# A blocked recurrence loop with its copies in another order, its last inversion product in the next group and its masks behind the solution's copy

## What is computed

```python
def step(S, inp):
    r_t, w_t, k_t, v_t, ma_t, b_t = inp
    sa = jnp.einsum('dbhij,dbhj->dbhi', S, ma_t)
    S = S * w_t[..., None, :] + sa[..., None] * b_t[..., None, :] + v_t[..., None] * k_t[..., None, :]
    return S, jnp.einsum('dbhij,dbhj->dbhi', S, r_t)
s_last, ys = lax.scan(step, s0, xs)
```

## Time and profile before

| | us |
|---|---|
| median of 3 runs | 2169.68 |
| lowest, highest | 2169.28, 2173.42 |
| the profiled execution | 2169.53 |
| its span in the trace | 2167.7 |
| its mean granted TensorE clock | 0.924 of full |

### The profile page before, as it was taken

The page is one execution under the profiler, slowest core; times in us unless marked ns, Lnnn a source line. Parts: engine busy times, 40 slices in busy tenths (PEclk is TensorE's granted clock), DMA queues, the critical chain, the costliest instruction groups (busy, mean ns, idle before and its releaser), DMA issues. The chain is left out here.

```text
span 2167.7 us, 55496 instructions
## 1 busy us (share of the span) xinstructions
PE 1842.1 (85%) x24160; PEld 1149.9 (53%) x24160; DVE 1038.4 (48%) x1685; ACT 633.9 (29%) x1233; POOL 524.9 (24%) x596
## 2 busy tenths in 40 slices
PE   6289577789999468999988379799999999999988
PEld 1234476335555258888888244355545455554533
DVE  8789566420888724555545644332221222212276
ACT  0511244322555323444444213231112121120202
POOL 0510000232111024555544433231202121120110
PEclk9589699889999779999999679899999999999999
DMA  6574332511344443333343222211111121111122
GB/s 232 218 210 174 122 110 80 182 43 41 118 151 152 140 156 96 105 103 101 95 143 91 100 100 98 107 57 60 40 39 40 39 78 39 40 39 39 40 74 92
DMA packets 172362, 215.87 MB, mean 100 GB/s; under 512 B 41035, under 2 KB 127051, under 8 KB 170447
## 3 DMA queue, kind: packets, MB, share of 16 engines
q1 hardware_dynamic: 172244, 214.18, 29.9%
HBM read 151.63 MB, written 60.42 MB: 98 GB/s over the span
## 5 line engine op out<-in xcount | busy, mean ns | idle before, releaser
L89 PE MATMUL psum<-arena 128*128 128x384 bf16 (+1 forms) x2028 | 711.5, 351 | 71.2 <-PEq L500 14.7
L90 PE MATMUL psum<-arena 128*128 128x384 bf16 (+1 forms) x2028 | 710.9, 351 | 0.0
L91 PE MATMUL psum<-arena 128*128 128x384 bf16 (+1 forms) x2028 | 710.2, 350 | 0.0
L1625 PE MATMUL psum<-arena 64*64 64x64 f32 x9216 | 347.5, 224 | 39.2 <-issue 32.6
L89 PEld LDWEIGHTS psum<-arena 128*128 128x128 bf16 x2028 | 201.1, 99 | 267.5 <-issue 41.2
L1625 PEld LDWEIGHTS psum<-arena 64*64 64x64 f32 x9216 | 312.4, 136 | 56.4 <-issue 51.3
L1619 PE MATMUL psum<-arena 64*64 64x64 f32 (+2 forms) x6336 | 286.5, 238 | 56.6 <-DMA arena<-xrec 38.5
L91 PEld LDWEIGHTS psum<-arena 128*128 128x128 bf16 x2028 | 201.3, 99 | 178.9 <-issue 9.0
L90 PEld LDWEIGHTS psum<-arena 128*128 128x128 bf16 x2028 | 201.3, 99 | 171.8 <-issue 7.6
L1619 PEld LDWEIGHTS psum<-arena 64*64 64x64 f32 x6336 | 245.5, 135 | 63.5 <-issue 60.8
L1752 ACT ACTIVATE arena<-psum 128x192 f32<-128x192 f32 (+2 forms) x624 | 173.3, 334 | 293.5 <-PE psum L1625 186.8
(11 more groups left out here) (274 smaller groups left out, 2006.2 us busy)
## 6 DMA issues: line engine op xcount, KB each, us to landing
arena<-in_w_ff SPq DMA_DIRECT2D x16, 2048.0 KB, 7.8
arena<-in_w_ada SPq DMA_DIRECT2D x12, 2048.0 KB, 8.4
arena<-xrec SPq DMA_DIRECT2D x72, 320.0 KB, 3.3
arena<-s_tab SPq DMA_DIRECT2D x8, 1600.0 KB, 7.4
x<-arena SPq DMA_DIRECT2D x18, 512.0 KB, 2.6
xrec<-arena SPq DMA_DIRECT2D x4, 2304.0 KB
arena<-xrec SPq DMA_DIRECT2D x72, 128.0 KB
arena<-x SPq DMA_DIRECT2D x18, 512.0 KB, 3.3
```

Source lines behind the costliest of these rows:

```text
L89: nc.tensor.matmul(out, whi, xhi, start=first, stop=False)
L90: nc.tensor.matmul(out, wlo, xhi, start=False, stop=False)
L91: return nc.tensor.matmul(out, whi, xlo, start=False, stop=last)
L1625: done = nc.tensor.matmul(out[half[1 - h]], lhs[half[h]], rhs[half[h]], start=first, stop=last)
```

## The change

It has three parts, though the few words for it name only the first.

1. ACT's copies of a level (1 to 4) go X of direction 0, X of direction 1, transpose of direction 0, transpose of direction 1, where they were X, transpose, X, transpose.
2. `update(5)` is gone. A new step `inverse()` stands in the next body right after `right_side(0)` and ahead of `start(0)`: 12 `heads` products (two directions, three chunks, two heads) into bank SUM, and one ACT copy of 128x384 for both directions in place of two of 128x192. `start(d)` now waits for `q_read` of level 5 and `xt` of level 4; `inverse` also waits for `lt`.
3. DVE's mask of the late matrices moves. For chunk 1 it stays in `right_side(0)`; for chunk 2 and chunk 0 of the next group it now stands in `solve(1)` and `solve(2)`, behind the copy of u.

```diff
@@ order
         if recur:
             f.right_side(0)
+            f.inverse()
...
             f.between(5)
-            f.update(5)
@@ PE
                         if j == 0:
-                            for d in D2:
-                                pe.wait_ge(ev("xt", LEVELS, d), ic)
+                            pe.wait_ge(ev("inv"), ic)
...
                         if recur:
-                            pe.wait_ge(ev("xt", LEVELS, d), ic)
+                            pe.wait_ge(ev("q_read", LEVELS, d), ic)
+                            pe.wait_ge(ev("xt", LEVELS - 1, d), ic)
...
+                    def inverse():
+                        for d in D2:
+                            pe.wait_ge(ev("ready"), 1)
+                            pe.wait_ge(ev("q_read", LEVELS, d), ic)
+                            pe.wait_ge(ev("xt", LEVELS - 1, d), ic)
+                        if chain:
+                            for d in D2:
+                                pe.wait_ge(ev("lt", d), ia)
+                        for d in D2:
+                            for j in G3:
+                                at = 2 * CK + CHAIN * d + CK * j
+                                last = heads(ps[:, SUM, at:at + CK], qs[d][:, j], xx[d][:, 1, j])
+                        last.then_inc(ev("xq", LEVELS), 1)
@@ ACT
                         for d in D2:
                             act.wait_ge(ev("xq", l, d), ia)
-                            if l < LEVELS:
-                                copy(pair(d)[:, 0], ps[:, CROSS[d], 0:CHAIN]).then_inc(ev("x", l, d), 1)
-                                copy(pair(d)[:, 1], ps[:, STAY[d], 0:CHAIN]).then_inc(ev("xt", l, d), 1)
-                            else:
-                                if recur:
-                                    act.wait_ge(ev("u", GROUP - 1), ic)
-                                copy(inv[d].rearrange("p j c -> p (j c)"), ps[:, STAY[d], 0:CHAIN]).then_inc(ev("xt", l, d), 1)
+                            copy(pair(d)[:, 0], ps[:, CROSS[d], 0:CHAIN]).then_inc(ev("x", l, d), 1)
+                        for d in D2:
+                            copy(pair(d)[:, 1], ps[:, STAY[d], 0:CHAIN]).then_inc(ev("xt", l, d), 1)
+
+                    def inverse():
+                        act.wait_ge(ev("xq", LEVELS), ic)
+                        copy(both_inv, ps[:, SUM, 2 * CK:2 * CK + 2 * CHAIN]).then_inc(ev("inv"), 1)
@@ DVE
                     def right_side(j):
-                        nxt = (j + 1) % GROUP
-                        if late0 if nxt == 0 else True:
-                            Part.late(nxt)
+                        if j == 0:
+                            Part.late(1)
...
                         nc.vector.tensor_copy(flat(u), ps[:, OFF, 2 * CK:4 * CK]).then_inc(ev("u_read", j), 1)
+                        if j == 1:
+                            Part.late(2)
+                        if j == 2 and late0:
+                            Part.late(0)
```

More of the change, by code:

```diff
@@ L1385, in stage_recurrence @@
     early = A.take(GROUP, 2, 2, CK)
+    CHAIN = GROUP * CK
     mt = [A.take(2, 5, CK) for _ in G3]
@@ L1390, in stage_recurrence @@
     xx = [A.take(2, GROUP, CK) for _ in D2]
-    inv = [A.take(GROUP, CK) for _ in D2]
+    both_inv = A.take(2 * CHAIN)
+    inv = [both_inv[:, d * CHAIN:(d + 1) * CHAIN].rearrange("p (j c) -> p j c", j=GROUP) for d in D2]
     qs = [A.take(GROUP, CK) for _ in D2]
@@ L1399, in stage_recurrence @@
     flat = lambda v: v.rearrange("p d c -> p (d c)")
-    CHAIN = GROUP * CK
     LATE, OFF, SUM = 4, 6, 7
@@ L1591, in update @@
                         pass
+                    def inverse():
+                        pass
                     def advance(j):
@@ L1730, in update @@
                                 at = slice(j * CK, j * CK + CK)
-                                if l < LEVELS:
-                                    across(ps[:, CROSS[d], at], xx[d][:, 1, j], qs[d][:, j])
+                                across(ps[:, CROSS[d], at], xx[d][:, 1, j], qs[d][:, j])
                                 last = heads(ps[:, STAY[d], at], qs[d][:, j], xx[d][:, 1, j])
                             last.then_inc(ev("xq", l, d), 1)
+                    def inverse():
[11 more added lines that the diff above has]
+                        last.then_inc(ev("xq", LEVELS), 1)
                     def early():
```

## The result

| | before | after |
|---|---|---|
| median of 6 runs each, us | 2170.39 | 2147.83 |
| lowest, highest | 2169.28, 2176.47 | 2137.70, 2152.80 |
| the profiled execution | 2169.53 | 2147.13 |
| its span | 2167.7 | 2145.3 |
| first u copy of the trace | 787.63 | 795.60 |

What follows compares the result with a forecast made beforehand. PE, busy 15.46 of a 16.97 us period, executes in order and idles where its queue's head waits. 22 turns x 0.6 + 21 masks x 0.8 - 1.4 = 28.6 us; 2169.5 - 28.6 = 2141 us, range 2134 to 2150 (chance 0.75).

Steps and rivals of the forecast that it cites:

- The turn: At the loop's turn, update(5) becoming inverse() lets right_side(0) start earlier: 0.6 us less per turn, 0.3 to 0.75.
- The mask of chunk 2: Behind u's copy in solve(1), it frees DVE for between(2)'s adds, so update(2) starts 0.8 us earlier, 0.61 to 0.85.
- the adds run from 909.80: At between(2), DVE's identity adds start at 909.80, behind the first product group's end at 909.77, without the mask ahead.
- The mask of chunk 0: Behind u's copy in solve(2), it delays between(4)'s adds, but advance(2) covers that: 0, upper bound 0.4 us.
- The order of the copies: On ACT, direction 1's X comes earlier, but PE has other products in front or gains little: 0, bound 0.2 us a period.
- How often: Over the recurrence, 22 turns at 0.6 and 21 masks at 0.8 count, less 1.4 lost at a load: 28.6 us.
- The yrec loads: The two loads issued at 1109.57 hold right_side(2), so that group's 0.6 + 0.8 us is lost; wait grows to about 3.5.
- Half of it: Rival: either the turn gives nothing (2153.5 us) or the displaced mask holds the new state (2157 us); chance 0.12.
- Loads: Rival: right_side(2) waits for its load in each period, keeping up to 0.8 us of it: 2153 us; chance 0.03.
- The copies alone: Rival: moved products and masks are hidden anyway, only ACT's copy order matters: 2165 to 2170 us; chance 0.04, with all hidden.
- Slower: PE's clock: Rival: new waits bring 1.2 GHz into steady periods, about 8 us each; six such periods give 2189 us; chance 0.04.
- What would show it: Trace signs: period 15.6 us, no PE idle over 0.2 ahead of update(2), right_side(0) within 0.3 of between(5), two waits grow.

Runs made afterwards that it cites:

- e1: Kernel before with only update(5) turned into inverse(), masks and ACT's copies as before; 2159.49 us, ratio 0.9953.
- e2: Kernel before with only DVE's masks moved; 2154.81 us, ratio 0.9939.
- e10: Kernel after with the mask of chunk 0 put back in right_side(2), ahead of u's copy; 2146.27 us, ratio 0.9887.
- e12: Kernel after with the new order of ACT's copies at level 3 alone, the old order at levels 1, 2 and 4; 2149.10 us, ratio 0.9893.
- e8: Kernel after, unchanged, traced and timed once more; 2147.38 us, ratio 0.9891.
- e4: Kernel after with ACT's copies back in the old order at all levels; 2147.57 us, ratio 0.9894.
- e5: Kernel after with the two yrec loads issued one each behind the first load_step in the last column tile's first two groups; 2141.51 us, ratio 0.9863.
- e3: Kernel before with only the order of ACT's copies changed; 2168.11 us, ratio 0.9998.
- e7: Kernel before with the yrec loads split over two groups and the large loads spread over the first tile's six groups; 2162.68 us, ratio 0.9967.
- e9: Kernel after with the new order of ACT's copies at level 4 only, the old order at levels 1 to 3; 2149.56 us, ratio 0.9903.
- e11: Kernel after with inverse()'s one 128x384 copy as two of 128x192; 2148.53 us, ratio 0.9906.

## Why the prediction was right, and where it was off

**The period** was forecast at 15.6 and is 15.56: 1.41 saved instead of 1.40. But its terms were off in ways that cancel: 0.2 too much for the mask, 0.22 too little for the order of the copies. That the period comes out to 0.04 is in part luck.

**The turn**, taken at 0.6 (0.3 to 0.75), is 0.62 alone (e1). Its steps: `right_side(0)` was to come 0.22 behind `between(5)` and comes 0.24 behind it (0.35 with the old copies); from there to u of chunk 0 was put at 3.16 (919.44 to 922.6) and is 3.19 (903.21 to 906.40).

**The mask of chunk 2**, taken at 0.8 (0.61 to 0.85), is 0.60 (e2). The step that failed is "the adds run from 909.80". That took the end of the last product's record of `between(2)` as the moment from which DVE could start, which made the first add 3.61 behind u of chunk 0; in e2 it is 908.48 - 904.59 = 3.89. In after the last product of that half of `between(2)` ends, by its record, at 909.79, and the add, with DVE idle in front of it, starts at 910.10. Behind `between(1)` this distance is 0.04. At `between(2)` the 64x192 products of `right_side(1)` stand directly ahead in PE's queue, and the last of them ends, by its record, only at 909.92. The profile says that ends of products are modelled, and the Trainium skill (Perfetto Trace Analysis, Summary: the profiler window per engine type) states that for TensorE the reported end is an estimate and the semaphore's way is not in it; the 0.31 here beside 0.04 there is in line with it. That the wider products make the difference is not shown, as no run moved them. The rows before had a sign of it: the mask, with 1.62 of idle in front, waited for products that stand ahead of `between(2)` in PE's queue, and it began only at 909.95, so the adds behind those products could hardly have begun at 909.80. `update(2)` therefore comes (908.95 - 904.59) 4.36 behind u of chunk 0 in e2, where 4.14 was forecast and 4.95 stood before. Two signs were in the prediction's own text: u itself was put only 0.66 earlier, and the lower bound of 0.61 was the measured idle, which is what came.

**The mask of chunk 0**, taken at 0: right (e10, 15.55 beside 15.56; e2 has its third stretch at 7.59 beside 7.58).

**The order of the copies**, taken at 0 with 0.2 as the bound: wrong, 0.10 alone and 0.22 with the rest. The step that failed is "at update(1), (2) and (4) it has right_side(1), advance(1) or early in front". For `update(4)` that looked at PE's products alone; the change had brought the branch of the loop right behind `between(5)`, and a branch waits until the sequencer has handed out everything ahead of it. At `update(3)` the same text found the 0.1 to 0.2 and rounded it to nothing; e12 has 0.11.

**How often.** By the prediction, the 23 periods between the first u copies shrink by 28.6: 0 in the first, 1.4 in each of 20, 0 at the yrec loads, 0.6 in the last. Measured between the two traces: 0.80 in the first, 1.35 in the second, 18 x 1.405 = 25.3 in the steady ones, 1.25 in the last but one; and against it -2.46 at the yrec loads (19.09 to 21.55) and -1.03 in the last (19.19 to 20.22). Sum 25.2; the lengths in the table give 25.3. The last period lies between 19.0 and 20.8 in the traces of all kernels, in no order, and stays open. Outside the recurrence the pair of traces lost 8.0 ahead of it and gained 5.1 behind it, by code that is the same in both: 25.3 - 8.0 + 5.1 = 22.4, the difference of the spans. The 5.1 goes with the granted clock (84 us at 1.2 GHz behind in before, 74 in after); the 8.0 stays open.

**The yrec loads** are the term that was sized wrongly. The wait was forecast to grow to about 3.5 and is 3.63; that it comes so close is luck, since the same kernel has 4.00 in e8, and others with the same gains have 3.07 to 4.76. What was not forecast is that the granted clock is then 1.2 GHz for a while. A windows view of after behind the wait, to be held against 1109.88 to 1128.97 of before, where the clock is 1.00 all through:

```profile
1103.30:1107.00 3.70, 3.70 (x91) 3.51 (x93) 0.00 (x0) 0.61 (x2) 0.00 (x0) 0.50 0.02 5
```

```profile
1109.88:1128.97 19.09, 15.50 (x648) 14.60 (x648) 8.67 (x27) 7.20 (x27) 8.77 (x20) 1.00 0.68 221
```

PE is busy for 17.65 us in this period of after instead of 15.3. The period is 5.99 longer than a steady one: 3.63 of wait and these 2.4. The Trainium skill (TensorE: Matmul & The Clock Gate, HAM oscillation — how this bites in real kernels) says that waits for transfers between bursts of products let the clock fall, so that the next burst starts slow; the trace of after agrees, while e4 had a wait of 3.10 and kept its clock (see the last section). e5, which takes the wait away, takes the slow stretch away too.

**The rivals.** "Half of it" did not come: both halves were there (e1, e2). "Loads" did not: right_side(2) has no idle ahead of it in a steady period. "The copies alone" fell with e3, which can't be told from before. "Slower: PE's clock" put the danger in the steady periods, and there the clock is 1.00; the rule about short idles that it names from the Trainium skill (TensorE: Matmul & The Clock Gate, A second HAM failure mode: psum-queue depth-cycling) is not borne out by the idles of this case. The lower clock appeared at the long wait, where the sum had set 0. One reading in that rival is wrong: the clock did not fall behind the idle of 5.02. In before it was at 1.2 GHz already ahead of this idle, which begins at 801.2:

```profile
797.20:801.00 3.80, 2.92 (x77) 2.92 (x77) 1.22 (x5) 0.83 (x3) 0.74 (x2) 0.50 1.03 418
```

**What would show it.** The period, the adds, the idle ahead of `update(2)` and the start of `right_side(0)` came as stated, but u stands 0.53 behind the first add and not 0.7. Of the two waits that were to grow, the second did; the first shrank from 5.02 to 4.37, while a gap in written-out code some 7 us ahead of it grew from 2.80 to 3.40, so that the two together stayed (7.82 and 7.77).

## What to carry to other kernels

When an engine that works in order is some 90% busy, look for the few idles at the head of its queue and take them away one by one. Each was worth about what the trace showed as idle: the mask 0.60 for 0.61, the turn 0.62 for 0.50 and 0.22, of which 0.24 stayed. Take the shown idle as the value, and the end of a TensorE record as a bound only. When a step is moved across the turn of a loop, ask again what the sequencer must hand out before the branch; and when a kernel gets faster, its waits for loads that don't move can grow (here from 2.08 to between 3.07 and 4.76), and may cost clock besides, so move those loads too.

## What the runs showed of the hardware that was not expected

- Behind the wait for the yrec loads, which every kernel but e5 to e7 has, the granted clock falls or doesn't, and not by the length of the wait alone. The third column is the mean granted clock in the 8 us from the end of the wait (windows view), the fourth the length of the period less that of a steady one:

| wait of PE, us | kernel | granted clock behind it | the period is longer by |
|---|---|---|---|
| 2.08 | before | 1.00 | 2.12 |
| 2.16 | e3 | 0.79 | 3.48 |
| 2.45, 2.58 | e1, e2 | 1.00 | 2.48, 2.65 |
| 3.10 | e4 | 1.00 | 3.09 |
| 3.07, 3.09, 3.15 | e9, e10, e11 | 0.83, 0.79, 0.79 | 4.38, 4.37, 4.41 |
| 3.63 | after | 0.65 | 5.99 |
| 4.00 | e8 | 0.79 | 5.36 |
| 4.76 | e12 | 0.67 | 6.95 |

  Where the clock stayed, the period is longer by the wait and nothing else. Where it fell, it is longer by 1.3 to 1.4 more (at about 0.8) or 2.2 to 2.4 more (at about 0.66). The rows of e4 and of e10, with waits of the same length:

```profile
1100.86:1108.86 8.00, 7.63 (x310) 7.31 (x314) 3.62 (x11) 2.83 (x11) 2.25 (x5) 1.00 0.28 76
```

```profile
1103.92:1111.92 8.00, 7.79 (x277) 7.61 (x279) 3.46 (x10) 2.77 (x10) 1.10 (x3) 0.79 0.19 45
```

- An identity add starts 0.30 to 0.31 behind the modelled end of its product at `between(2)` (e2, e4, after), where 64x192 products stand directly ahead of that product in the queue, and 0.04 behind it at `between(1)`, where none do.
- The branch of PE's loop, 0.2 us long, starts in these traces only when the last waited group has been handed out, and the next body's first product comes 0.7 to 0.8 behind its start (920.15 to 920.86 in before, 902.50 to 903.21 in after, 897.91 to 898.67 in e4); an idle of 0.24 is left at the turn in after.
